# Stores of the new token rows: issued where the rows are made, or in the prompt attentions' blocks

## The reference, cut to what matters

```python
# layer 0 (forgetting attention, "FoX", 8 heads x 64)
q, k, v, f, u = split(h @ w_in)
k = rms_norm(k, k_norm)                       # returned: fox_k, fox_v, one row of 512 per token
# layer 1 (native sparse attention, "NSA", 4 KV heads x 64, three branches)
q, kc, vc, ks, vs, kw, vw, gl = split(h @ w_in)
kc, ks, kw = (rope(rms_norm(a, g), pos) for a, g in ...)
# returned: nsa_kc, nsa_vc, nsa_ks, nsa_vs, one row of 256 per token,
# and nsa_kw, nsa_vw: a window buffer, 508 old rows and the 4 new ones per sample
```

## Time and profile before

| | us |
|---|---|
| median of 3 runs | 2777.14 |
| lowest and highest | 2760.77 and 2780.5 |
| the profiled execution, whole | 2772.47 |
| its span, first to last instruction | 2770.8 |
| PE busy in the span | 2269.3 (82%) |
| DVE, ACT, POOL busy | 1202.7, 581.4, 270.4 |
| moved by the 16 DMA engines | 321.92 MB, mean 116 GB/s |
| mean granted clock of PE | 0.890 of 2.4 GHz |

### The profile page before, as it was taken

One profiled execution on the slowest core, in us unless ns is written; L12 is line 12 of the kernel. 1 busy time (PEld: TensorE's weight loads), 2 busy tenths in 40 slices (PEclk: granted clock), 3 DMA queues, 4 the chain that ended last, 5 costly groups with the idle time before them and its releaser, 6 DMA issues. The chain is left out here.

```text
span 2770.8 us, 46037 instructions
## 1 busy us (share of the span) xinstructions
PE 2269.3 (82%) x16993; PEld 1961.9 (71%) x16993; DVE 1202.7 (43%) x2134; ACT 581.4 (21%) x999; POOL 270.4 (10%) x433
## 2 busy tenths in 40 slices
PE   3983546776999898896669896999997766999898
PEld 2862432355999898793468785777885456999898
DVE  4314721135444432425355554556543345444432
ACT  2101111002111000201125354445441212111000
POOL 0010223300000000000012122112110310000000
PEclk7995778788999999897679798999998998999999
DMA  6651059962223221223200004223233841233221
GB/s 254 217 195 44 0 197 386 384 249 96 84 83 91 87 85 57 69 69 140 95 1 1 1 1 126 88 92 122 71 113 139 308 143 54 86 89 86 91 96 56
DMA packets 238575, 321.92 MB, mean 116 GB/s; under 512 B 17851, under 2 KB 196104, under 8 KB 230959
## 3 DMA queue, kind: packets, MB, share of 16 engines
q1 hardware_dynamic: 211671, 199.44, 22.1%
q0 software_dynamic: 26720, 120.09, 11.8%
HBM read 311.56 MB, written 16.42 MB: 118 GB/s over the span
## 5 line engine op out<-in xcount | busy, mean ns | idle before, releaser
L381 PE MATMUL ps<-XHup,WHup 128*128 128x272 f32 x1408 | 293.4, 290 | 28.8 <-DVE XLup L357 25.3
L381 PE MATMUL ps<-XHup,WLup 128*128 128x272 f32 x1408 | 292.9, 290 | 0.0
L381 PE MATMUL ps<-XLup,WHup 128*128 128x272 f32 x1408 | 291.8, 289 | 0.0
L381 PEld LDWEIGHTS ps<-XHup,WHup 128*128 128x128 f32 x1408 | 223.1, 190 | 30.8 <-DVE XLup L357 26.8
L1954 PE MATMUL ps<-CHi,W1H 128*128 128x512 f32 (+1 forms) x512 | 207.5, 405 | 19.6 <-DVE CLo L2023 19.6
L381 PEld LDWEIGHTS ps<-XLup,WHup 128*128 128x128 f32 x1408 | 222.8, 190 | 0.0
L381 PEld LDWEIGHTS ps<-XHup,WLup 128*128 128x128 f32 x1408 | 221.3, 190 | 0.0
L2023 DVE TENSOR_TENSOR CLo<-RAWc,CHi 128x512 fp32r<-128x512 f32 x128 | 139.8, 1113 | 163.4 <-ACT CHi L1977 163.4
L1955 PE MATMUL ps<-CLo,W1H 128*128 128x512 f32 (+1 forms) x512 | 205.6, 402 | 0.0
L1956 PE MATMUL ps<-CHi,W1L 128*128 128x512 f32 (+1 forms) x512 | 204.7, 400 | 0.0
L1977 ACT CAST CHi<-RAWc 128x512 fp32r<-128x512 f32 x128 | 143.1, 1155 | 155.4 <-PE ps L1956 136.0
(11 more groups left out here) (458 smaller groups left out, 4163.4 us busy)
## 6 DMA issues: line engine op xcount, KB each, us to landing
RAWup<-in_w_up SPq DMA_DIRECT2D x88, 512.0 KB, 3.9
Wmod<-in_w_mod POOLq DMA_DIRECT2D x20, 2048.0 KB, 10.7
VP<-in_cache_fox_v POOLq DMA_DIRECT2D x128, 256.0 KB, 6.0
KP<-in_cache_fox_k SPq DMA_DIRECT2D x128, 256.0 KB, 10.4
RAWdn<-in_w_down SPq DMA_DIRECT2D x14, 1408.0 KB, 6.4
RAWin<-in_nsa_w_in SPq DMA_DIRECT2D x20, 512.0 KB, 3.6
KS<-in_cache_nsa_ks SPq DMA_DIRECT2D x80, 128.0 KB, 2.9
Wmod<-in_w_mod SPq DMA_DIRECT2D x4, 2048.0 KB, 19.1
```

Of the source, the lines that this page charges most:

```text
L381: mm = self.nc.tensor.matmul(self.ps[:, banks + n, 0:HALF], w, x[:, n * HALF:(n + 1) * HALF], start=start, stop=stop)
```

## The change

`to_tokens` only makes the rows and has no SP stream. A new `store_tokens` issues the same DMAs and then waits until all have landed. `prompt_attention` gets a parameter `store`, which an SP stream of its block calls. In layer 1 the wait for `copied` goes there too, `TOK` is lent by the outer stage (so it stays until after `nsa_prompt`), `stored` is cleared with the outer stage's semaphores, and the inner stage has no semaphores left, so that it ends without a clearing block.

```diff
-    def to_tokens(self, PT, first, n, TOK, stores, st):
+    def to_tokens(self, PT, first, n, TOK):
...
-                @block.sync
-                def _(sp):
-                    evacuated(sp, len(units))
-                    for name, c, width, row in stores:
-                        sp.dma_start(o[name + "_p"]..., TOK[:, 0:4, c:c + width]).then_inc(st, 16)
...
+    def store_tokens(self, sp, TOK, stores, st):
+        o, count = self.o, 0
+        for name, c, width, row in stores:
+            sp.dma_start(o[name + "_p"]..., TOK[:, 0:4, c:c + width]).then_inc(st, 16)
...
+            count += 1 + (NB if row else 1)
+        sp.wait_ge(st, 16 * count)
...
-    def prompt_attention(self, T, sems, groups, heads, keysets, outs, setup_dve):
+    def prompt_attention(self, T, sems, groups, heads, keysets, outs, setup_dve, store):
...
         with nc.Block() as block:
+            @block.sync
+            def _(sp):
+                store(sp)
...
 # fox_mixer
-                stores = self.to_tokens(PT, 4, 8, TOK, [("fox_k", 0, 512, 0), ("fox_v", 512, 512, 0)], stored)
+                self.to_tokens(PT, 4, 8, TOK)
                 self.pooling(PT)
-                self.fox_prompt(PT, TOK, NC)
+                self.fox_prompt(PT, TOK, NC, lambda sp: self.store_tokens(sp, TOK, [...], stored))
                 with nc.Block() as block:
-                    @block.sync
-                    def _(sp):
-                        sp.wait_ge(stored, 16 * stores)
...
 # cmp_prompt
-                @block.sync
-                def _(sp):
-                    for semaphore, value in waits:
-                        sp.wait_ge(semaphore, value)
...
 # nsa_mixer
-                copied, w_in = sem2("window_copied"), sem2("cmp_w_in")
+                copied, w_in, stored = sem2("window_copied"), sem2("cmp_w_in"), sem2("tok_stored")
...
-                with self.stage() as (sbt, semt):
-                    W1, TOK, stored = sbt("W1", [P, 2, 16, 256]), sbt("TOK", [P, 5, 1536]), semt("tok_stored")
+                TOK = sb2("TOK", [P, 5, 1536])
+                with self.stage() as (sbt, _):
+                    W1 = sbt("W1", [P, 2, 16, 256])
...
-                self.nsa_prompt(PT, VE, GT, KCP, VCP)
+                def store(sp):
+                    self.store_tokens(sp, TOK, [...the same six...], stored)
+                    sp.wait_ge(copied, 32)
+                self.nsa_prompt(PT, VE, GT, KCP, VCP, store)
```

More of the change, by code:

```diff
@@ L879, in _ @@
                             nc.vector.scalar_tensor_tensor(px, px, CT[:, g:g + 1], two((6, 0)[t % 2]), ALU.mult, ALU.mult).then_inc(scaled, 1)
[L882 to L886 removed]
+    def to_tokens(self, PT, first, n, TOK):
+        nc, ps = self.nc, self.ps
         with self.stage() as (sb, sem):
@@ L925, in _ @@
                     copy(dve, 1)
-                @block.sync
-                def _(sp):
-                    evacuated(sp, len(units))
-                    for name, c, width, row in stores:
[L931 to L938, removed]
+    def store_tokens(self, sp, TOK, stores, st):
+        o, count = self.o, 0
+        for name, c, width, row in stores:
+            sp.dma_start(o[name + "_p"][0, 0].rearrange("(t p) h d -> p t (h d)", p=P), TOK[:, 0:4, c:c + width]).then_inc(st, 16)
+            rows = o[name + "_s"][0].rearrange("b t h d -> b t (h d)")
+            for b in range(NB if row else 1):
+                if row:
+                    sp.dma_start(rows[b, row:row + TS, :], TOK[b * TS:(b + 1) * TS, 4, c:c + width]).then_inc(st, 16)
+                else:
+                    sp.dma_start(rows.rearrange("b t f -> (b t) f"), TOK[0:NS, 4, c:c + width]).then_inc(st, 16)
+            count += 1 + (NB if row else 1)
+        sp.wait_ge(st, 16 * count)
     def forget(self, NC, EP):
@@ L1334, in _, with fox_prompt @@
                         nc.gpsimd.tensor_tensor(dst, dst, T2[:, adds[g] % 2, :, :], ALU.add).then_inc(sems["added"], 1)
-    def fox_prompt(self, PT, TOK, NC):
+    def fox_prompt(self, PT, TOK, NC, store):
         nc, H = self.nc, self.H
@@ L1364, in fox_prompt @@
                                    value=lambda j, h=h: VE[:, j, h, :]))
-            self.prompt_attention(T, sems, groups, heads, keysets, [H[:, c, 0:TP] for c in range(4)], setup)
+            self.prompt_attention(T, sems, groups, heads, keysets, [H[:, c, 0:TP] for c in range(4)], setup, store)
     def gather(self, pool, table, col, where, dst, loaded):
@@ L1555, in fox_mixer @@
                 self.head_norm(PT, [(t, 76 + t // 4) for t in range(8)], False)
-                stores = self.to_tokens(PT, 4, 8, TOK, [("fox_k", 0, 512, 0), ("fox_v", 512, 512, 0)], stored)
+                self.to_tokens(PT, 4, 8, TOK)
                 self.pooling(PT)
-                self.fox_prompt(PT, TOK, NC)
+                self.fox_prompt(PT, TOK, NC, lambda sp: self.store_tokens(sp, TOK, [("fox_k", 0, 512, 0), ("fox_v", 512, 512, 0)], stored))
                 with nc.Block() as block:
-                    @block.sync
-                    def _(sp):
-                        sp.wait_ge(stored, 16 * stores)
                     @block.vector
@@ L1765, with cmp_prompt @@
     CMP_SEMS = ("ea", "ed", "hid", "gx", "gs", "gu", "gt", "gh", "w2", "dc")
-    def cmp_prompt(self, PT, c, KCP, VCP, waits):
+    def cmp_prompt(self, PT, c, KCP, VCP):
         nc, ps, n = self.nc, self.ps, TP // STRIDE
@@ L1801, in _, with nsa_prompt @@
                     nc.vector.tensor_copy(VCP[:, :], ps[0:n - 1, 3, 0:4 * HD])
-    def nsa_prompt(self, PT, VE, GT, KCP, VCP):
+    def nsa_prompt(self, PT, VE, GT, KCP, VCP, store):
         nc, H = self.nc, self.H
@@ L1838, in nsa_prompt @@
                         heads.append(dict(src=PT[own, gp * 4 + r, 0:TP], own=own, other=other))
-            self.prompt_attention(T, sems, groups, heads, keysets, [H[:, c, 0:TP] for c in range(8)], setup)
+            self.prompt_attention(T, sems, groups, heads, keysets, [H[:, c, 0:TP] for c in range(8)], setup, store)
     def key_pages(self, engine, b, dst, full):
@@ L2399, in nsa_mixer @@
                     self.head_norm(PT, tiles, True, lambda sp: self.nsa_loads(sp, W1, W2, PR, w_in, copied))
-                    keep = 512 - TS
-                    stores = self.to_tokens(PT, 8, 12, TOK, [("nsa_kc", 0, 256, 0), ("nsa_vc", 256, 256, 0), ("nsa_ks", 512, 256, 0),
-                                                             ("nsa_vs", 768, 256, 0), ("nsa_kw", 1024, 256, keep), ("nsa_vw", 1280, 256, keep)], stored)
+                    self.to_tokens(PT, 8, 12, TOK)
                     self.prepare_compression(W1, W2, PB, PR, w_in, PT, TOK, QS, KN, VN, VE)
@@ L2406, in nsa_mixer @@
                                  XG=sb3("XGp", [P, 2, 124]), UG=sb3("UGp", [P, 2, 124]), HID=sb3("HIDp", [P, 2, 124]))
-                        self.cmp_prompt(PT, c, KCP, VCP, [(stored, 16 * stores), (copied, 32)])
-                self.nsa_prompt(PT, VE, GT, KCP, VCP)
+                        self.cmp_prompt(PT, c, KCP, VCP)
+                def store(sp):
+                    keep = 512 - TS
+                    self.store_tokens(sp, TOK, [("nsa_kc", 0, 256, 0), ("nsa_vc", 256, 256, 0), ("nsa_ks", 512, 256, 0), ("nsa_vs", 768, 256, 0),
+                                                ("nsa_kw", 1024, 256, keep), ("nsa_vw", 1280, 256, keep)], stored)
+                    sp.wait_ge(copied, 32)
+                self.nsa_prompt(PT, VE, GT, KCP, VCP, store)
             with self.stage() as (sb4, sem4):
```

## The result

The changed kernel takes 2754.4 us (2743.6 to 2759.9) where the kernel before takes 2777.1 (2760.8 to 2784.5) in the same rounds on the same chip. The ratio is 0.992, with an interval of 0.990 to 0.994: about 22 us less, which is inside the 1% that I had called no measurable change, and measurable after all with nine executions of each. In microseconds the interval reaches from 16 to 28.

The account below looks back on a forecast made before the run. PE was taken to bound the whole, SP's DMA issuing the two store phases; 14.0 + 3.5 + 0.8 + 2.0 + 2.5 = 22.8 us off gave 2749.7 (profiled execution) or 2754.3 (median), put at 2752, range 2733 to 2768.

Parts of the forecast that it names:

- SP's issuing holds the blocks: Store phases of both layers: SP's DMA issuing keeps the blocks open; removing it gains 14.0 us in layer 1, 3.5 in layer 0.
- The higher price of 1.59: Alternative crossing time between blocks, in us; with it the issuing gains would be 13.5 in layer 1 and 2.8 in layer 0.
- The cover: Prompt attentions: SP only waits there, so issuing and landing of the stores are hidden with over 60 us to spare.
- nothing added in the attentions: Both prompt attentions: the 30 DMA issues, the wait and the transfers beside compute cost zero.
- Rival three: Both attentions: stores delay code fetch, each attention begins only when they are through, 22 us given back, 2774; chance 0.04.
- PE's clock in prepare_compression: Layer 1's products L1665 run at 2.4 GHz instead of 1.2 after a shorter pause: 2.5 us less, bounds 0 and 2.5.
- Pooling: Layer 0: loads SR and MAP no longer queue behind stores, MAP lands 2.6 us earlier; gain 2.0, bounds 0 and 2.0.
- Rival two: Only issue time and the clearing block go, pooling and PE's clock stay: 18.3 us gained, 2756; chance 0.12.
- The clearing block: Between cmp_prompt and nsa_prompt in layer 1: one clearing block falls away, gaining 0.8 us, bounds 0.5 and 1.2.
- Rival one: NSA's attention: unsteady slow clock stretches of 19.4 us decide; one fewer 0.20, one more (2771) 0.08, two more (2791) 0.03.
- the case with one stretch fewer: NSA's attention: the median has one slow clock stretch fewer, 19 us less than 2752, giving 2733; chance 0.20.

## Why the prediction was right, and where it wasn't

**SP's issuing holds the blocks** (14.0 and 3.5): right, 14.22 and 3.60. I took the same crossing's 1.05 and 0.97; it was 0.84 in both layers, and so in each later trace with the stores out of the way. The higher price of 1.59, from a block with 14 semaphores, didn't apply. The experiment with the stores in the next block shows the condition from the other side: the gain is the issuing time less what the new block can't cover, and there 7.7 was not covered.

**The cover** (60 us and more to spare) and **nothing added in the attentions**: right. The spare time in the shorter attention is 69.2 still, and leaving the stores out gains nothing. Rival three's reasoning, that an attention's new code would have to come past the stores, has no effect that shows in its own place: 14.20 against 14.19, 8.86 against 8.86.

**PE's clock in prepare_compression** (2.5, bounds 0 and 2.5): right in size in the profiled execution, 2.48, and in cause, as the transposes in the pause show. But the same kernel's second trace has 0.8, so the 2.5 was the upper bound and not to be had in each execution: three of eight traces miss 1.7 of it. My row had hinted at it. It showed a granted 1.00 up to 1350, and the products were to begin at 1349.4 and to run for more than 3 us. I also hadn't said that it can be a loan from what follows: in the old order with the pause filled half of it went again in cmp_prompt. In the changed kernel cmp_prompt is 0.24 shorter, so there it stayed.

**Pooling** (2.0, bounds 0 and 2.0): the mechanism is right, the size was off, and the high end with it. The profile shows 2.85. Of that, 2.09 come up to DVE's copy L1079 and belong to MAP, as with the loads issued first (2.02). MAP landed 3.3 us after its issue and not the 2.6 that I had taken from another load, so that 0.64 of DVE's wait is left. DVE's first copy does follow 1.07 instead of 1.77 after PE's start, since PE came in at the high clock, but those 0.7 were spent waiting for MAP. The remaining 0.8 are the products L1063, 5.47 instead of 6.26, for which the sum had no term. They come with the loads' new place too (5.52), pause or no pause, and why isn't shown. Rival two (neither pooling nor the clock moves, 18.3) is out by the ledger for the executions profiled, and for pooling by every trace with the loads in front; for the clock's 2.5 it holds in part in those three traces.

**The clearing block** (0.8, bounds 0.5 and 1.2): mis-sized, 0.39, below my lower bound. I had divided 2.10 by putting 1.3 on cmp_prompt's own crossing with 10 semaphores, interpolated between 0.87 and 1.59; that crossing takes 1.71. The row of 0.87 holds a whole crossing and a clearing block with it, so it was no price of a clearing block alone.

**Rival one** (the clock in the attention decides, "I see no cause in this program"): its premise was the weakest step. The stretch isn't a thing of single executions. It stands at the same two heads in all ten traces, behind a pause that DVE's key making causes, and it can be made shorter by an edit. The cause was to be read in the kernel before: the same four DVE instructions, the same 4.3 us wait. I had looked at what PE did before the clock fell in stretches of whole heads, where a pause of 4 us doesn't show. The 0.20 that I gave the case with one stretch fewer was therefore too much; the range was wider on that side than the traces warranted. What spreads the executions of one kernel over 16 us isn't this stretch, whose two heads differ by 3 us over the ten traces. Differences lie in many stages (over all traces the part behind layer 1's attention ranges from 1073 to 1093), and what makes them stays open.

The time itself, 2754.4 against 2752, came out because the errors in the sum (+0.85 and -0.4, and up to -1.7 for the clock) are small beside the 17.5 us of issuing, which one view shows outright. How close it came is partly luck. The choice between the profiled execution's 2749.7 and the median's 2754.3 mattered as much; a difference worked out in one execution belongs on the median.

## What to carry to other kernels

A block, or any place where all engines meet, lasts as long as its slowest queue, and issuing DMAs is work for a queue: 26 issues cost 14 us here with no engine computing. Put issues whose data isn't needed soon into a block that is longer than the issuing, and not simply into the next one; price a pause of PE with the lower clock of the products behind it as well, as a bound and not as a sure gain, for executions of one kernel differ in it. One trace is one execution: read a term of 2 us in a second one before calling it right. And where a clock stretch looks like chance, look whether it begins at the same instruction in each trace, and read the few microseconds before it row by row.

## What the runs showed of the hardware

- Issuing from SP took 14.0 us for 26 stores, between 0.3 and 1.1 us for one, with the engines standing still (before) and beside the attention (after). Beside `prepare_compression` it took 14.8, with 1.9 for one of them.
- The granted clock stayed at 1.00 under transposes alone (116 in 12.88 us), and it was still 1.00 when products began 1.5 us after a crossing of 0.84. In three of eight traces it fell to 0.50 right as these products began, behind the same gap of PE of 3.0 us.
- After a pause of PE of 4.3 us in the middle of dense work the clock came to 0.50 and stayed there for some 16 us (1511 to 1528), and it fell once more in the same two heads, which took 48.4 instead of 29.8 us. Without that pause they still took 37.5, so a second cause is left.
- The same DVE subtraction of 64x512 took 0.68 us alone and 1.00 and 1.66 where POOL's cast (1507.04) and subtraction (from 1507.75 to 1509.34) ran beside it. The Trainium skill (SBUF — State Buffer, Who interferes with whom) has a DVE instruction with two SBUF inputs contend with a GpSimd instruction that reads SBUF, over a pair of ports that they share and that one of them locks. The trace agrees: the 1.66 begins at 1508.22 under POOL's subtraction and ends 0.54 after it, and the 1.00 begins at 1507.21 under POOL's cast and ends 0.54 after that one (1507.67).
